# RMS norms over the features in a two-block network: sums of squares on all partitions, root and reciprocal on a row of 256

## What is computed

```python
def _rmsnorm(x, g):
    xf = x.astype(jnp.float32)
    y = xf * lax.rsqrt(jnp.mean(xf * xf, axis=-1, keepdims=True) + NORM_EPS)
    return (y * g.astype(jnp.float32)).astype(x.dtype)
...
        x = x + gt_m[:, None] * _rmsnorm(merged @ w_out[layer], g_mix_post[layer])
        h2 = _rmsnorm(x, g_ffn_pre[layer]) * (1.0 + sc_f[:, None]) + sh_f[:, None]
...
    for layer in range(DEPTH_2):
        h = rms_norm(x, norm_mix_pre[layer])
        m = mixer_block(h, ...)
        x = x + rms_norm(m, norm_mix_post[layer]).astype(x.dtype)
        h = rms_norm(x, norm_ffn_pre[layer])
        f = swiglu(h, w_ffn_gate[layer], w_ffn_up[layer], w_ffn_down[layer])
        x = x + rms_norm(f, norm_ffn_post[layer]).astype(x.dtype)
```

## Time and profile before

| | us |
|---|---|
| median of 3 runs | 2854.43 |
| lowest, highest | 2853.51, 2856.98 |
| the profiled execution | 2863.69 |
| its span in the trace | 2861.5 |
| PE busy in the span | 2530.3 (88%) |
| DVE busy | 536.6 (19%) |
| ACT busy | 566.0 (20%) |
| POOL busy | 341.8 (12%) |

### The profile page before, as it was taken

The page is one execution under the profiler, slowest core; times in us unless marked ns, Lnnn a source line. Parts: engine busy times, 40 slices in busy tenths (PEclk is TensorE's granted clock), DMA queues, the critical chain, the costliest instruction groups (busy, mean ns, idle before and its releaser), DMA issues.

```text
span 2861.5 us, 29944 instructions
## 1 busy us (share of the span) xinstructions
PE 2530.3 (88%) x12500; PEld 1632.1 (57%) x12500; DVE 536.6 (19%) x1150; ACT 566.0 (20%) x827; POOL 341.8 (12%) x99
## 2 busy tenths in 40 slices
PE   3999987779999899999998889989799799887997
PEld 2478636543333333333333377767799677776997
DVE  1002214321111211111112121013122120123231
ACT  2102311121111111111111101121243111122332
POOL 4000000000000000000000000002287000011774
PEclk7996967869999999999999989989899899888998
DMA  9343350329999989999999586621245757311442
GB/s 227 114 147 112 123 206 16 111 114 410 398 391 391 408 359 392 409 400 389 391 408 399 215 225 136 160 89 59 80 171 177 198 97 176 118 59 59 153 167 94
DMA packets 137557, 625.77 MB, mean 219 GB/s; under 512 B 11169, under 2 KB 23073, under 8 KB 112641
## 3 DMA queue, kind: packets, MB, share of 16 engines
q1 hardware_dynamic: 132480, 622.02, 59.2%
q10 hardware_dynamic: 3872, 2.26, 0.4%
q0 software_dynamic: 1120, 0.23, 0.4%
HBM read 623.26 MB, written 1.05 MB: 218 GB/s over the span
## 4 chain that ended last, share of the span: by engine, by line
PE 84%; DVE 7%; ACT 4%; issue 2%; DMA 2%; DVEq 0%; ACTq 0%; SPq 0%
PE bank L1001 26%; PE bank L1277 24%; PE bank L1509 8%; PE bank L1524 4%; PE bank L1270 2%; PE bank L1317 2%; PE bank L1016 2%; PE bank L1344 2%; DMA ring<-in_w_ada 1%; PE bank L1067 1%; PE bank L963 1%; PE bank L1303 1%; DVE arenaA L1841 1%; DVE arenaA L1846 1%; DVE arenaA L1843 1%
## 5 line engine op out<-in xcount | busy, mean ns | idle before, releaser
L1001 PE MATMUL bank<-arenaA,ring 128*128 128x256 f32 (+1 forms) x3200 | 749.6, 396 | 28.2 <-ACT arenaA L649 9.2
L1001 PEld LDWEIGHTS bank<-arenaA,ring 128*128 128x128 f32 x3200 | 624.6, 196 | 149.6 <-issue 47.5
L1277 PE MATMUL bank<-ring,arenaA 128*64 128x512 f32 x3072 | 702.6, 611 | 6.6 <-ACT arenaA L797 6.6
L1277 PEld LDWEIGHTS bank<-ring,arenaA 128*64 128x64 f32 x3072 | 217.1, 140 | 471.1 <-issue 458.4
L2035 POOL TENSOR_TENSOR ring_rounded<-ring,ring_rounded 128x2048 fp32r<-128x2048 f32 (+1 forms) x76 | 311.6, 4128 | 703.8 <-ACT ring_rounded L891 703.8
L1509 PE MATMUL bank<-arena_rounded,ring_rounded 128*128 128x256 f32 x2112 | 255.4, 284 | 8.0 <-ACT arena_rounded L904 8.0
L1509 PEld LDWEIGHTS bank<-arena_rounded,ring_rounded 128*128 128x128 f32 x2112 | 255.0, 192 | 8.6 <-issue 8.6
L2027 POOL DMA_DIRECT2D arenaA<-in_gla_w_a x2 | 1.0, 512 | 1739.5 <-DVE xT L1744 1578.8
L817 ACT ACTIVATE arenaA<-bank 128x512 f32<-128x512 f32 (+1 forms) x96 | 56.8, 591 | 573.8 <-PE bank L1001 429.0
L891 ACT ACTIVATE ring_rounded<-ring 128x2048 fp32r<-128x2048 f32 (+1 forms) x76 | 124.1, 1681 | 230.9 <-PE bank L1001 94.1
L1524 PE MATMUL bank<-arena_rounded,ring_rounded 128*128 128x256 f32 x1056 | 127.6, 283 | 3.2 <-ACT ring_rounded L891 3.2
(11 more groups left out here) (342 smaller groups left out, 1792.2 us busy)
## 6 DMA issues: line engine op xcount, KB each, us to landing
ring<-in_w_gate SPq DMA_DIRECT2D x64, 2048.0 KB, 9.1
ring<-in_w_lin SPq DMA_DIRECT2D x64, 2048.0 KB, 11.1
ring<-in_w_down SPq DMA_DIRECT2D x64, 2048.0 KB, 10.2
ring<-in_w_in SPq DMA_DIRECT2D x39, 2048.0 KB, 15.2
ring<-in_w_ada SPq DMA_DIRECT2D x12, 2048.0 KB, 8.1
ring<-in_w_ffn_gate SPq DMA_DIRECT2D x10, 2048.0 KB, 8.9
ring<-in_w_ffn_up SPq DMA_DIRECT2D x10, 2048.0 KB, 7.8
ring<-in_w_ffn_down SPq DMA_DIRECT2D x12, 1536.0 KB, 6.6
```

The costliest lines, as they stand in the source:

```text
L1001: last = pe.matmul(dst, w[:, c, base + m * P:base + (m + 1) * P], rhs(c), start=(c == 0), stop=(c == kc - 1))
L1277: last = pe.matmul(bank[b][k * SLOTS:(k + 1) * SLOTS, :], lhsT(c), slot(j)[:, c % 4, k * 512:(k + 1) * 512], start=(c == 0 and bias is Non ...
```

## The change

Step 2 now uses 128 columns of ones as weights, and all eight chunks add up in the same 128x256 region of bank 6, so the sum of squares of each token is there on every partition at once. Steps 3, 4 and 6 are gone: the copy, the `pick` matmuls and the matmuls with the identity. Step 5 runs on `nrow`, 128x256 in place of `ncol`, 128x2: mean + eps from bank 6 by DVE, the root by ACT, the reciprocal by DVE, in place. `row` is now `nrow` in SBUF. The three functions `norm` in the diff are those of ACT, of PE and of DVE, in this order.

```diff
             def norm(k, src, before=None):
...
-                act.wait_ge(n_par, k + 1)
-                act.activation(nrow, bank[6][:, 0:T], ACT.Copy).then_inc(n_parc, 1)
                 act.wait_ge(n_ms, k + 1)
-                act.activation(ncol[:, :], ncol[:, :], ACT.Sqrt).then_inc(n_root, 1)
+                act.activation(nrow, nrow, ACT.Sqrt).then_inc(n_root, 1)
...
             def norm(k, n0):
                 for c in range(DC):
                     if c % 4 == 0:
                         pe.wait_ge(n_sq, k * 2 + (c // 4 + 1))
-                    r = 32 * (c % 4)
-                    last = pe.matmul(bank[6][r:r + 32, 0:T], ones[:, 0:32], sq2[:, c, :], start=(c < 4), stop=(c >= 4),
-                                     skip_group_check=True)
-                last.then_inc(n_par, 1)
-                pe.wait_ge(n_parc, k + 1)
-                for t in range(TT):
-                    last = pe.matmul(bank[6][:, t:t + 1], nrow[:, t * P:(t + 1) * P], K["pick"][:, 0:1], start=True, stop=True)
+                    last = pe.matmul(bank[6][:, 0:T], ones[:, 0:P], sq2[:, c, :], start=(c == 0), stop=(c == DC - 1))
                 last.then_inc(n_sum, 1)
-                pe.wait_ge(n_col, k + 1)
-                for t in range(TT):
-                    last = pe.matmul(bank[7][:, t * P:(t + 1) * P], ncol[:, t:t + 1].to_broadcast([P, P]), K["ident"][:, :],
-                                     start=True, stop=True)
-                last.then_inc(n_row, 1)
...
             def norm(k):
                 dve.wait_ge(n_sum, k + 1)
-                dve.tensor_scalar(ncol[:, :], bank[6][:, 0:2], 1.0 / D, EPS, ALU.mult, ALU.add).then_inc(n_ms, 1)
+                dve.tensor_scalar(nrow, bank[6][:, 0:T], 1.0 / D, EPS, ALU.mult, ALU.add).then_inc(n_ms, 1)
                 dve.wait_ge(n_root, k + 1)
-                dve.reciprocal(ncol[:, :], ncol[:, :]).then_inc(n_col, 1)
+                dve.reciprocal(nrow, nrow).then_inc(n_row, 1)
                 dve.wait_ge(n_row, k + 1)
-            row = bank[7][:, 0:T]
+            row = nrow
```

## The result

The changed kernel takes 2875.06 us (median of 20 runs, 2862.97 to 2885.80) against 2860.74 us before (20 runs, 2849.35 to 2867.03). The ratio of the two is 1.0057, with a 95% interval of 1.0043 to 1.0071: slower by 12 to 20 us. The forecast was slower by 24.3 us, with 2864 to 2888 us as its range. That 2875.06 us lies only 3.6 us from the forecast's 2878.7 us is partly luck: the forecast stood on a median of three runs, 2854.43 us, and over 20 runs the kernel before takes 6.3 us more.

A forecast was written before the change was run, and what follows sets the result against it. PE bounds the kernel: busy 88% of the span, chain of waits on it 84%. Dearer sum matmuls, +32.0 us, less a shorter tail, -7.7, give +24.3 us; on the 2854.43 us median, 2878.7 us, range 2864 to 2888 us (70%).

The forecast's parts named there:

- The matmuls of the sum: Summing the squares in all eleven norms: full-width passes, mostly at the low clock, cost +32.0 us together.
- The six runs from a low clock: Norms 0, 2, 3, 6, 7, 10: passes take 5.6 us against 2.0, +3.6 us each, +21.6 us.
- the three in two bursts: Norms 1, 5, 9: one dense run of 5.6 us against 4.0, +1.6 us each, +4.8 us.
- norms 4 and 8: Norms starting at the high clock: 4.8 us, midway between 6.1 and 3.6, against 2.0; +5.6 us together.
- most of this work is at the low level: Sum passes of all eleven norms before the change: claimed to run mostly at the low clock, 1.2 GHz.
- the allowance I had made: Top of range: clock rising 0.8 us later than in two projections, +0.4 us in nine norms, 3.6 us.
- The tail: From last pass to the row's first use: 2.8 us against 3.5, -0.7 us in each of eleven, -7.7 us.
- (a): Rival: the clock never rises in a norm, runs take 7.2 us; +41 us, 2896 us; 7%.
- (b): Rival: the clock is high throughout the norms; +8 us, 2862 us; 10%.
- (c): Rival: the reciprocal costs no more than other operations, 1.3 us less in eleven norms; +10 us, 2864 us; 5%.
- (d): Rival: full-width passes raise the clock and it holds until PE's next work; -17 us, 2837 us; 4%.
- (e): Rival: added time hidden behind weight loads; MoE loads could hide norms 0 and 1, 3.8 us; 4%.

The follow-up runs named there:

- The first experiment: Only the sum's matmuls made full width, everything behind them as in the kernel before, against that kernel: ratio 1.0087, 2886.77 us against 2855.45.

## Why the prediction was right, point by point

**The matmuls of the sum: right in size, by terms that missed on both sides.** +31.4 us against the forecast's +32.0. The six runs from a low clock gave +22.4 (forecast 21.6), the three in two bursts +5.5 (4.8), norms 4 and 8 +3.4 (5.6). The last is a mis-sized term: I took the middle between a clock that is held and one that falls as before, and it was held in both. In the three other kernels with wide f32 passes it was held in both as well. That it is the denser passes that hold it is not shown all the same: with only the wide tail the passes in column groups of norms 4 and 8 ran at the high clock as well. And in the kernel before it fell only when half of the passes of norms 4 and 8 were through, so the prediction's "most of this work is at the low level" does not hold for these two. In the other direction norms 0 and 1 ran at the low clock for 5.6 and 5.8 us, longer than the 3.7 and 4.0 us that I had from two projections and outside the allowance I had made; norms 3 and 7, where it rose 4.1 and 4.8 us in, took 5.7 and 6.1 us. In norms 2, 5, 6, 9 and 10, at 5.4 us each, it rose 3.4 to 3.6 us in, a little earlier than in either row. The wide sum alone costs the same 59.3 us of runs, and fp32r passes take the cost away.

The trace had eight passes at 1.08 us in groups against 3.5 us wide at the low clock. The Trainium skill ("TensorEngine Tiling (Array Packing)", section Theoretical Speedup) promises up to four times from column tiles. The trace agrees with the direction. The runs grew 1.4 to 3.2 times and not four: in the ones that started low the clock rose on the way, in norms 4 and 8 it was held, and in norms 1, 5 and 9 the run before held a wait for the second square already, 1.8 us of the 3.98 us in norm 5.

**The tail: right in size, with a wrong reason for part of it.** -8.1 us against -7.7; 0.42, 0.42 and 1.75 us are what the rows gave. The reciprocal at 1753 ns is 6.2 ns for each element beyond two, the slope between 2 and 8 elements in the earlier trace rows. The Trainium skill ("VectorE: DVE Perf Modes", section First, the fixed hardware budget) has a repeat count of 8 for its divide. Taken as eight cycles for each element, which is an estimate from that page, it would have been 2.3 us; the measured 6.2 ns are six cycles of that page's 0.96 GHz, and the measurement decides. But the forecast booked the 0.7 us as what the removal of three steps is worth. The first experiment shows that behind a wide sum those steps would have been as fast as their replacement. What the tail's change is worth by itself depends on the clock: behind column groups, where the wide pick has to be added, it is 0.9 us dearer a norm.

**What the forecast left out: the loop's turn.** The prediction named the branch as what delays norms 3 and 7, and costed nothing there. For norm 3 the rows say ACT's late squares, as shown above. The prediction said that the removed matmuls sit on the path; it did not ask what PE does in the time that becomes free. PE left the norm earlier, and the wait at the turn moved beside the tail: -4.0 us at norm 7, confirmed by holding PE back (+3.5 us), and -0.7 us at norm 3, for which holding PE back changed nothing, as ACT sets the time there; why ACT came earlier is open. Together they are most of the 6.2 us by which the +18.1 us of the profile fall short of +24.3.

**Rivals.** (a) and (b) are refuted as general cases: the clock rose in nine runs and was high throughout in two. (c) falls with 1753 ns. (d) needed a clock that holds over PE's wait behind a norm. It did hold for some us: behind the last norm it is still 1.00 from 2855 to 2857 us, 4 us after the last pass. But PE's wait is 8.70 us there, and its next matmuls start low and take little less than the 3.68 us of the earlier trace rows (first the timeline, then PE's window):

```profile
2861.51 3.38 PE L1517 MATMUL bank<-k_ident,xT 128*128 128x128 f32 x16 [8.70 <-DVE xT L1854]
...
2861.50:2864.00 2.50, 2.49 (x12) 0.50 0.00 0
```

(e) The gap between norms 1 and 2, experts included, did not shrink, so the delay of norms 0 and 1 wasn't hidden. It grew by 1.0 us, as it did in the kernels whose norms 0 and 1 were as short as before (1061.3 and 1061.4 us), so that is not the delay either.

## What to carry to other kernels

In nine of the eleven norms here the matmuls behind PE's wait ran at the low clock from within 0.3 us of their start, so price such matmuls at that level, and ask whether their length carries them over the rise; short work in column groups or in one pass was cheaper here than dense work through which the clock rises late. When instructions leave an engine's program, look at what that engine does next, branches included: a wait that the profile calls "issue" can move off the path, by an amount that has to be measured. And a mechanical gain measured behind one kind of work (the tail behind a low-clock sum) is not the gain behind another.

## What the runs showed of the hardware that I had not expected

- With nearly the same instructions ahead of it, norm 0 starts between 551.4 and 563.6 us in the profiles of eight kernels; the mean granted clock over the 240 us from 250 on was 0.79 in the profile before and 0.85 in the one after. Times of this kernel can only be compared over many runs, or over a stretch.
- PE took 7.2 to 9.6 us from its last matmul ahead of the loop's turn to its first behind it in the kernels where no other engine sets that time, and at most 6.9 us in the changed one.
- Matmuls on constant operands with an unread result kept the clock high where they reached to within 1.1 us of the next matmuls; where 3.4 to 3.5 us of waiting remained, it stayed high through one norm and fell 0.5 and 0.9 us into two others. The time they won ahead of the norms was not to be found in the end result, while the ones behind the sums came with a profile 9 us shorter.
